# Keys and heads turned in 32x32 squares by VectorE and put together through DRAM, instead of turned by TensorE

## What is computed

```
h = rms_norm(x, norm_g) * (1 + scale) + shift
proj = h @ w_in                        # columns: u, z_pool, q, k, v, o, z_mlstm, gates
pool_out = causal_pool_mixer(u) * silu(z_pool)
q, k = silu(causal_depthwise_conv(q | k))
...
# mLSTM, 4 heads of 128, chunks of 128 positions, state C carried from chunk to chunk
dmat = exp(d_log - m_t[..., None])
s = einsum('bhtd,bhsd->bhts', q, k) * dmat
num = einsum('bhts,bhsd->bhtd', s, v) + inter[..., None] * einsum('bhvd,bhtd->bhtv', C, q)
h = num / maximum(abs(den), exp(-m_t))[..., None]
C_new = decay[..., None, None] * C + einsum('bhs,bhsv,bhsd->bhvd', w, v, k)
...
hm = hm * rsqrt(mean(hm * hm) + EPS) * mh_norm_g * sigmoid(o) * silu(z_mlstm)
x = x + gate * (concat(pool_out, hm) @ w_out)
return rms_norm(x, final_g)
```

## Time and profile before

| | |
|---|---|
| median of 3 runs | 1834.39 us (1833.92 to 1835.27) |
| the profiled execution's own time | 1837.02 us |
| its span, from the first to the last instruction | 1835.2 us |
| mean granted TensorE clock | 0.993 of full speed |
| TensorE busy | 98% of the span |
| VectorE busy | 57% |
| ScalarE / GpSimd busy | 32% / 14% |
| SP's queue, share of the 16 DMA engines' time | 55.2% |

### The profile page before, as it was taken

How to read it: one execution, slowest core, us unless ns; L and a number is a source line. 1 busy time by engine, 2 the same in 40 slices (tenths; PEclk the granted TensorE clock), 3 DMA queues, 4 the chain that set the end, 5 groups by cost and what they waited for, 6 DMA issues and landing times.

```text
span 1835.2 us, 25120 instructions
## 1 busy us (share of the span) xinstructions
PE 1792.8 (98%) x9369; PEld 1537.8 (84%) x9369; DVE 1037.0 (57%) x2249; ACT 582.2 (32%) x1334; POOL 264.7 (14%) x229
## 2 busy tenths in 40 slices
PE   5999999999999999999999999999999999999998
PEld 5877778888898888988888888888889888898886
DVE  6685586435846178352773448552683627835383
ACT  3245343332423224222342224332241313422221
POOL 3443123040210003000130001300021000300000
PEclk9899999999999999999999999999999999999999
DMA  9796754587356754667536674467545575366431
GB/s 328 259 330 177 207 159 138 194 283 227 103 188 191 186 193 102 207 199 181 173 93 232 204 199 125 154 197 201 199 113 181 187 197 186 101 207 199 152 120 69
DMA packets 256797, 336.85 MB, mean 184 GB/s; under 512 B 129100, under 2 KB 171044, under 8 KB 256676
## 3 DMA queue, kind: packets, MB, share of 16 engines
q1 hardware_dynamic: 241476, 312.57, 55.2%
q10 hardware_dynamic: 15200, 22.68, 4.3%
HBM read 288.86 MB, written 46.33 MB: 183 GB/s over the span
## 4 chain that ended last, share of the span: by engine, by line
PE 87%; DVE 7%; issue 2%; ACT 2%; SPq 1%; DMA 1%; POOL 0%; ACTq 0%; DVEq 0%; POOLq 0%
PE ps_acc L536 23%; PE ps_acc L538 23%; PE ps_acc L537 23%; PE ps_kv L536 2%; PE ps_kv L537 2%; PE ps_kv L538 2%; PE ps_sco L728 1%; PE ps_num L748 1%; PE ps_kv L752 1%; PE ps_num L747 1%; PE ps_num L536 1%; PE ps_num L538 1%; PE ps_num L537 1%; DVE sb_acc_cv L1513 1%; PE ps_bro L760 1%
## 5 line engine op out<-in xcount | busy, mean ns | idle before, releaser
L536 PE MATMUL ps_acc<-sb_hT_hi,sb_w_split 128*128 128x512 f32 x1536 | 609.7, 397 | 3.6 <-POOL sb_w_split L1148 3.6
L538 PE MATMUL ps_acc<-sb_hT_hi,sb_w_split 128*128 128x512 f32 x1536 | 599.8, 391 | 0.0
L537 PE MATMUL ps_acc<-sb_hT_lo,sb_w_split 128*128 128x512 f32 x1536 | 599.1, 390 | 0.0
L536 PEld LDWEIGHTS ps_acc<-sb_hT_hi,sb_w_split 128*128 128x128 f32 x1536 | 289.4, 188 | 62.5 <-POOL sb_w_split L1148 4.1
L538 PEld LDWEIGHTS ps_acc<-sb_hT_hi,sb_w_split 128*128 128x128 f32 x1536 | 288.9, 188 | 62.4
L537 PEld LDWEIGHTS ps_acc<-sb_hT_lo,sb_w_split 128*128 128x128 f32 x1536 | 289.5, 188 | 56.4
L1159 POOL TENSOR_TENSOR sb_h_rs<-sb_h_var,sb_mhalf 128x4 f32<-128x4 f32 x32 | 32.3, 1011 | 1062.7 <-DVE sb_h_var L1607 1062.7
L1148 POOL TENSOR_TENSOR sb_w_split<-sb_w_raw,sb_w_split 128x512 fp32r<-128x512 f32 (+1 forms) x64 | 88.5, 1392 | 195.6 <-ACT sb_w_split L825 195.4
L1513 DVE SCALAR_TENSOR_TENSOR sb_acc_cv<-sb_shifted,sb_par,sb_acc_cv 128x512 f32<-128x512 f32 x96 | 76.9, 801 | 61.0 <-ACT sb_acc_cv L994 58.5
L1539 DVE TENSOR_TENSOR sb_oz<-sb_tanh,sb_oz 128x512 f32<-128x512 f32 x32 | 22.2, 692 | 150.4 <-ACT sb_tanh L1010 150.4
L536 PE MATMUL ps_acc<-sb_wo_hi,sb_mixm_hi 128*128 128x512 f32 x256 | 101.8, 398 | 0.0
(11 more groups left out here) (226 smaller groups left out, 2979.1 us busy)
## 6 DMA issues: line engine op xcount, KB each, us to landing
sb_w_split<-w_kept SPq DMA_DIRECT2D x328, 512.0 KB, 3.9
sb_w_split<-w_kept SPq DMA_DIRECT2D x56, 520.0 KB, 4.7
w_kept<-sb_w_split SPq DMA_DIRECT2D x40, 512.0 KB, 5.6
sb_x_res<-x SPq DMA_DIRECT2D x34, 512.0 KB, 4.7
sb_w_raw<-w_in SPq DMA_DIRECT2D x64, 256.0 KB, 5.1
out<-sb_qT SPq DMA_DIRECT2D x32, 512.0 KB, 2.9
sb_x_in<-x SPq DMA_DIRECT2D x112, 128.0 KB, 4.0
sb_ada_raw<-w_ada SPq DMA_DIRECT2D x8, 1024.0 KB, 10.2
```

Source lines behind the costliest of these rows:

```text
L536: pe.matmul(dst, st_hi, mv_hi, start=start, stop=False)
L537: pe.matmul(dst, st_hi, mv_lo, start=False, stop=False)
L538: return pe.matmul(dst, st_lo, mv_hi, start=False, stop=stop)
```

## The change

TensorE turns neither keys nor heads any more. The tensor `kT` is laid out chunk by chunk. After each z tile VectorE turns one head of the keys in 32x32 squares into a free buffer (`keys_squared`), and SP writes the squares in pieces of 32 numbers to their places in a DRAM tensor `keys_kept` (`keep_keys`, four DMAs a head) and later loads whole rows back (`load_keys`, one DMA a chunk). The heads are turned in squares by VectorE (`head_turn`), written to DRAM in whole rows (`keep_hm`) and read back in pieces of 32 numbers (`load_hm`, four DMAs a chunk). VectorE's order in a chunk changes: the exponents (now one instruction, with the subtraction moved into four activations of ScalarE) come ahead of `update_c`, `head_norm` behind `q_in`, and `m_mixed` one chunk later. The core of the diff:

```diff
-B_USES = 9
+B_USES = 5
...
-        qT, kT, oz = sb("qT", [P, NH, BLK]), sb("kT", [P, NH, BLK]), sb("oz", [P, NH, BLK])
+        qT, kT, oz = sb("qT", [P, NH, BLK]), sb("kT", [P, NC, NH, P]), sb("oz", [P, NH, BLK])
...
+        keys_squared = [conv[1], conv[0], shifted[:, 0, HALO:], shifted[:, 1, HALO:]]
...
+            def keep_keys(b, h):
+                sp.wait_ge(keys_turned, b * NH + (h + 1))
+                squares = keys_kept[:, h, :].rearrange("(n b) (d a) -> d b n a", b=32, a=32)
+                for d in range(4):
+                    sp.dma_start(squares[d], keys_squared[h][32 * d:32 * d + 32, :].rearrange("b (n a) -> b n a", a=32)).then_inc(
+                        keys_kept_done, 16)
+
+            def load_keys(b, j):
+                dst = k_w[:, :, :]
+                if j == 0:
+                    sp.wait_ge(keys_kept_done, 256 * (b + 1))
+                    if b == 0:
+                        sp.wait_ge(fold_mm, 2 * NH)
+                else:
+                    sp.wait_ge(sco_full, b * SCO_FULLS + j)
+                    dst = kT[:, j - 1, :, :]
+                sp.dma_start(dst, keys_kept[P * j:P * j + P, :, :]).then_inc(keys_loaded[j % 2], 16)
+
+            def keep_hm(b, j):
+                sp.wait_ge(hm_turned, b * NC + (j + 1))
+                sp.dma_start(hm_kept[j % 2].rearrange("p (h n) -> p h n", h=NH), kT[:, j, :, :]).then_inc(hm_kept_done, 16)
+
+            def load_hm(b, j):
+                sp.wait_ge(hm_kept_done, 16 * (b * NC + (j + 1)))
+                squares = hm_kept[j % 2].rearrange("(t c) (h d r) -> c h t d r", c=32, h=NH, r=32)
+                for d in range(4):
+                    dst = kT[32 * d:32 * d + 32, j, :, :].rearrange("c h (t r) -> c h t r", r=32)
+                    sp.dma_start(dst, squares[:, :, :, d, :]).then_inc(hm_loaded, 16)
...
+                    if m in (33, 35, 37, 39):
+                        keep_keys(b, (m - 33) // 2)
+                    if m in (41, 45, 49, 53):
+                        load_keys(b, (m - 41) // 4)
+                    if m in (50, 54):
+                        keep_hm(b, (m - 50) // 4)
+                    if m in (51, 55):
+                        load_hm(b, (m - 51) // 4)
...
-                def keys_transposed(j):
-                    if first and j == 0:
-                        pe.wait_ge(wout_scaled, KT)
-                    reach(pe, c_done, b * NC + j)
-                    for h in range(NH):
-                        last = pe.transpose(kv[1][:, chunk(h)], kT[:, h, chunk(j)], ident)
-                    last.then_inc(k_T, 1)
...
-                def hm_transposed(j):
-                    bro_wait(5 + j)
-                    pe.wait_ge(hm_ready, b * NC + (j + 1))
-                    for h in range(NH):
-                        last = pe.transpose(bro[:, chunk(h)], hm[:, h, :], ident)
-                    last.then_inc(bro_full, 1)
...
-                    act.activation(dmat[:, :, :], dmat[:, :, :], ACT.Exp, scale=-1.0).then_inc(d_exp, 1)
+                    for h in range(NH):
+                        last = act.activation(dmat[:, h, :], dmat[:, h, :], ACT.Exp, scale=-1.0,
+                                              bias=a_pad[:, NH * j + h:NH * j + h + 1])
+                    last.then_inc(d_exp, 1)
...
+                    if 8 <= t < 12:
+                        in_turn()
+                        V.transpose(keys_squared[t - 8].rearrange("p (c n) -> p c n", n=P), kT[:, :, t - 8, :]).then_inc(keys_turned, 1)
+                        did(keys_turned, b * NH + (t - 7))
...
+                def head_turn(j):
+                    in_turn()
+                    V.transpose(kT[:, j, :, :], hm[:, :, :]).then_inc(hm_turned, 1)
+                    did(hm_turned, b * NC + (j + 1))
...
-                    V.tensor_tensor(k_w[:, :, :], kv[1][:, :].rearrange("p (h d) -> p h d", d=P),
-                                    rows(expo[:, 1, NH * j:NH * j + NH]), ALU.mult).then_inc(k_w_ready, 1)
...
+                    dve.wait_ge(keys_loaded[j % 2], 16 * (b * 2 + (j // 2 + 1)))
+                    V.tensor_tensor(k_w[:, :, :], kT[:, j - 1, :, :] if j else k_w[:, :, :], rows(expo[:, 1, NH * j:NH * j + NH]), ALU.mult).then_inc(k_w_ready, 1)
...
-                    if i == 1:
-                        m_mixed(3)
                     if i in (1, 3):
                         m_low(2 + i // 2)
+                    if i == 2:
+                        m_mixed(3)
```

More of the change, by code:

```diff
@@ L328, in hT_part, with by_chunk @@
             return t[:, 4 * half:4 * half + 4, chunk(c)].rearrange("p (a b) t -> p a b t", b=2)
+        def by_chunk(t):
+            return t.rearrange("p (c t) -> p c t", t=P)
         def col(t, n, m=P):
@@ L513, in one_block @@
                         load_w(b, m)
+                        if m == UNITS + 3:
+                            keep_hm(b, 2)
+                    load_hm(b, 2)
                     load_x(b + 1, 2)
+                    keep_hm(b, 3)
                     load_x(b + 1, 3)
+                    load_hm(b, 3)
                     load_w(b, UNITS)
+                else:
+                    for j in (2, 3):
+                        keep_hm(b, j)
+                        load_hm(b, j)
                 store(b, 0)
@@ L727, in heads_to_scores @@
                     for h in range(NH):
-                        last = pe.matmul(sco[:, chunk(h)], kT[:, h, chunk(j)], qT[:, h, chunk(j)], start=True, stop=True)
+                        last = pe.matmul(sco[:, chunk(h)], kT[:, j, h, :], qT[:, h, chunk(j)], start=True, stop=True)
                     last.then_inc(sco_full, 1)
-                def keys_transposed(j):
-                    if first and j == 0:
-                        pe.wait_ge(wout_scaled, KT)
-                    reach(pe, c_done, b * NC + j)
-                    for h in range(NH):
-                        last = pe.transpose(kv[1][:, chunk(h)], kT[:, h, chunk(j)], ident)
-                    last.then_inc(k_T, 1)
                 def numerator_and_update(j):
@@ L750, in numerator_and_update @@
                     pe.wait_ge(k_w_ready, b * NC + (j + 1))
+                    if first and j == 0:
+                        pe.wait_ge(wout_scaled, KT)
                     for h in range(NH):
@@ L1595, in update_c @@
                     dve.wait_ge(kv_done, b * NC + (j + 1))
-                    if j >= 2 and not last_block:
-                        dve.wait_ge(x_summed, b * NC + (j - 1))
                     for h in range(NH):
@@ L1669, in one_block @@
                         heads(j - 1)
-                        update_c(j - 1)
                     in_turn()
                     dve.wait_ge(m_row_loaded, 16 * (b * NC + (j + 1)))
-                    for h in range(NH):
-                        last = V.scalar_tensor_tensor(dmat[:, h, :], m_row_all[:, chunk(h)], a_pad[:, NH * j + h:NH * j + h + 1],
-                                                      bigm, ALU.subtract, ALU.add)
-                    last.then_inc(m_row_read, 1)
+                    V.tensor_tensor(dmat[:, :, :], m_row_all[:, :].rearrange("p (h t) -> p h t", t=P),
+                                    bigm.unsqueeze(1).broadcast_to([P, NH, P]), ALU.add).then_inc(m_row_read, 1)
                     did(m_row_read, b * NC + (j + 1))
+                    if j > 0:
+                        update_c(j - 1)
+                        head_var(j - 1)
+                    if j > 1:
+                        m_mixed(j - 2)
                     in_turn()
@@ L1686, in one_block @@
                     did(sco_free, b * S_USES + (SCO["qk", j] + 1))
-                    if j > 0:
-                        head_var(j - 1)
-                        head_norm(j - 1)
-                    if j == 3 and not last_block:
-                        prep_var(b + 1, 0)
                     in_turn()
@@ L1698, in one_block @@
                     did(q_in_ready, b * NC + (j + 1))
-                    dve.wait_ge(k_T, b * NC + (j + 1))
-                    V.tensor_tensor(k_w[:, :, :], kv[1][:, :].rearrange("p (h d) -> p h d", d=P),
-                                    rows(expo[:, 1, NH * j:NH * j + NH]), ALU.mult).then_inc(k_w_ready, 1)
+                    if j > 0:
+                        head_norm(j - 1)
+                    if j == 3 and not last_block:
+                        prep_var(b + 1, 0)
+                    in_turn()
+                    dve.wait_ge(keys_loaded[j % 2], 16 * (b * 2 + (j // 2 + 1)))
+                    V.tensor_tensor(k_w[:, :, :], kT[:, j - 1, :, :] if j else k_w[:, :, :], rows(expo[:, 1, NH * j:NH * j + NH]), ALU.mult).then_inc(k_w_ready, 1)
                     did(k_w_ready, b * NC + (j + 1))
                     if j > 0:
+                        head_turn(j - 1)
                         y_low(j - 1)
+                    if j == 0:
+                        dve.wait_ge(keys_kept_done, 256 * (b + 1))
                     windows(j)
@@ L1715, in one_block @@
                     y_mixed(j)
-                    if 0 < j < 3:
```

(1 more changed line is left out.)

36 lines of the change are left out of this document (21 added, 15 removed).

## The result

The changed kernel takes 1825.65 us (median of 4 runs, 1822.92 to 1827.28), the one before on the same chip 1834.83 (4 runs): a ratio of 0.995, 95% interval 0.9938 to 0.9962. It is 9 us faster. 28 were forecast, and the time lies above the range (1800 to 1821). The profiled execution took 1827.28 us by its own time, 9.74 less than the one of before.

A forecast was written before the change was run, and what follows sets the result against it. TensorE's total work was taken to bound the kernel: 1837.0 us less 28.2 of transposes gives 1808.8, all else at nothing. The profiled execution stood 2.6 above the median, so 1806 was forecast, range 1800 to 1821.

The forecast's parts named there:

- The 28.2 us of transposes: On TensorE, 64 groups of four key or head transposes at 0.44 us each go away, 3.5 us a block.
- Room in the z tiles: 22 us x (1 - 0.71) = 6.4 us free: In the z tiles, DMA engines have 6.4 us free a block for the keys' 7.4 us of short writes.
- the ring's 15.2 us: Weight loads are issued 19.1 us before use and land in 3.9, so may be 15.2 us late.
- Late by 3 to 5 us: under 15: Weight loads behind `keep_keys` in SP's queue come 3 to 5 us late, under the 15 allowed.
- The price of a piece, 14.5 ns: Each 128-byte piece written to DRAM takes 14.5 ns of one DMA engine, the price of reading x.
- second rival: The keys' short writes are dear, losing from 49 ns a piece on; 1871 us at 58 ns; slower: chance 0.09.
- third rival: The transposes on TensorE were hidden anyway, giving 1834 us; chance almost nothing.
- `m_mixed` needs the heads a chunk later, 14.5 us, against 4 + 3 + 4: In the chunk stage, heads have 14.5 us for writing 4, issuing 3 and reading 4; costed at nothing.
- net 0, bounds -4 and +10: Block 0: `zp` 0 about 3 us late, waits on VectorE saved later; net 0, from -4 to +10 us.
- VectorE at nothing: VectorE's added turns, 40 us, are covered by 14 us less exponents and saved idle time; cost nothing.
- 1.2 us is the upper bound: In each chunk, ScalarE's one exponential of 0.63 us becomes four, together at most 1.2 us.
- partial loss: VectorE partly stays the pace or block 0 is at its worst: 1811 to 1828 us, chance 0.18.

The follow-up runs named there:

- the two kernels without keys there: Against the changed kernel: keys turned by TensorE throughout, 1822.26 us; keys turned by TensorE in blocks 0 and 1 only, residual loads behind unit 52, 1811.54 us.
- the copy issued by ScalarE: Changed kernel with the keys' pieces written a second time into a DRAM tensor nobody reads, that second copy issued by ScalarE's queue: 1830.92 us.
- three moves: Against the changed kernel, on SP's queue: residuals behind unit 52, 1819.96; block 1's x loads later, 1822.07; block 0's first keys' load later, 1827.85; together 1815.64 us.
- the last kernel: Changed kernel with keys turned by TensorE in blocks 0 and 1, by VectorE and DRAM from block 2, residual loads behind unit 52: 1811.54 us.

## Why the prediction was wrong

- **The 28.2 us of transposes** were right: 29.8 by the steady blocks, 3.73 a block against 3.5.
- **"Room in the z tiles: 22 us x (1 - 0.71) = 6.4 us free"** is the step that failed, with the ring's 15.2 us behind it. The row is from block 2 and was used for every block. In block 1 the z tiles read 0.96 and the z and o tiles of the window 1.05: there is next to no room. The ring's 15.2 us are those of the eight-slot units and of a load that lands in 3.9 us; the load that came late is unit 43, of the five-slot ring, and it had about 6 us. It was issued 13.0 us late and cost 9.6 us, where the sum has nothing. That the keys cause it is shown by the two kernels without keys there (14.96 us); that added traffic does it even when SP issues none of it, by the copy issued by ScalarE (27.79). That the order counts as well shows in the x loads: behind unit 44 instead of 42 they cost chunk 0 nothing.
- **"Late by 3 to 5 us: under 15"** held in block 2 (some 2 us a head) and not in block 1 (3.4 to 6.0 a head, 17.6 together, and 3.6 more for x).
- **The price of a piece, 14.5 ns,** was about right. ScalarE's queue takes 7.6% of 16 engines' time with the keys on it and 4.2% without; the difference over 1825.5 us is 993 engine-us for 65536 pieces, 15.2 ns each. By what SP's queue takes less in that run (64.1 to 61.3%) it is 12.5. These are estimates from rounded shares. The share in block 2's z tiles rose to 0.87, not the 1.0 foretold, but a part of the keys falls into its o tiles, where it went from 0.87 to 0.98. The second rival, 49 ns, is dead: 16384 short writes a block cost blocks 2 to 6 nothing in chunk 0. The rule that the prediction cites from the Trainium skill (DMA: Bandwidth & Descriptors, Specifications), that under 512 bytes the engine reads, modifies and writes, shows no price twice that of short reads here. (Where the prediction says that it makes the "third rival" likelier, it can only mean the second.)
- **"`m_mixed` needs the heads a chunk later, 14.5 us, against 4 + 3 + 4"** left out what else stands in the queue there, the 1 MB of residuals: 6.1 us in blocks 1, 2, 3 and 5, and shown by moving it.
- **Block 0, "net 0, bounds -4 and +10":** 4.5 us, inside the bounds. `zp` 0 was late by 2.7, as worked out. Chunk 1 won 4.3 us against before, and chunk 2 lost 6.4 to late raw loads. Which transfer is at the root there stays open: three moves only shifted it, and the last kernel still waits 3.7 us.
- **VectorE at nothing:** right as to the order, worth 29.3 us, but with luck in the sum. VectorE's busy time rose by 41 us, not by 40 - 14 = 26: a turn takes 0.71 us, not 0.62, and the product of the heads and `oz` 0.91 on average, not 0.69. "1.2 us is the upper bound" for the four exponentials was low (1.28), and of the 2.1 us of idle time a chunk 1.5 went, not all.

What was left at nothing adds up to 9.6 + 6.1 + 4.5 = 20.2. On the scale of the profiled executions the forecast was 1808.8 and 1827.28 came, 18.5 more: that is the 20.2 less the 1.6 that the transposes gave above the sum. The time does lie where the prediction put a "partial loss" (1811 to 1828), but that was written for VectorE or block 0; block 0 is 4.5 us of it. What it named as a sign, waits on `w_split` with SP held up, is what happened.

## What to carry to other kernels

A window of free transfer time counts for its own stage and block alone: read the share in each block that differs (here the first two, which load raw weights and store them) before a transfer is called hidden. In an in-order queue, price what stands between a store and the load that brings it back, not only the two. Look up which ring and which place in the queue the load has that will be late first. And a change can be applied to the blocks that have room for it: together with the residuals moved, that version was 14 us faster than the whole change, 8.4 of it from the keys.
